# Tiles moved into the first rows of two attentions, a wait taken block by block, and a sigmoid moved by one row

## The reference, cut to what matters

```python
# first block, per layer
q, k, v, z_a, u_h, z_h, g_a, g_h = split(rms_norm(x) @ w_in)
p = softmax(q @ k.T + bias)                      # per head, two maps
o = (p[0] - lam * p[1]) @ v
y_a = rms_norm(o) * (1 - lam_init) * silu(z_a)
z = fft_long_conv(hv, filt[0]) * hx1
z = fft_long_conv(z, filt[1]) * hx2              # order 0, order 1
y_h = z * silu(z_h)
m = sigmoid(g_a) * (y_a @ w_pa) + sigmoid(g_h) * (y_h @ w_ph)
x = x + rms_norm(m @ w_out)
# second block, per layer
o_a = rmsnorm(gated_delta_rule(q, k, v, g, beta)) * silu(gz)
kv = rmsnorm(mkv) @ mla_w_ukv                    # key half kn, value half vv, per head
o_b = causal_softmax(qf @ kf.T) @ vm * silu(mz)  # eight heads, query blocks of 128
o_c = rg_lru(u) * silu(lz)
x = x + concat(o_a, o_b, o_c) @ w_out
```

## Time and profile before

| | us |
|---|---|
| median of 3 runs | 2236.86 (2232.17 to 2242.91) |
| the profiled execution | 2236.85 |
| its span, first to last instruction | 2234.8 |
| PE busy | 2137.4 |
| DVE / ACT / POOL busy | 1279.9 / 893.5 / 625.4 |
| mean granted clock of TensorE | 0.975 |

### The profile page before, as it was taken

The page is one execution under the profiler, slowest core; times in us unless marked ns, Lnnn a source line. Parts: engine busy times, 40 slices in busy tenths (PEclk is TensorE's granted clock), DMA queues, the critical chain, the costliest instruction groups (busy, mean ns, idle before and its releaser), DMA issues. The chain is left out here.

```text
span 2234.8 us, 25471 instructions
## 1 busy us (share of the span) xinstructions
PE 2137.4 (96%) x9696; PEld 1593.6 (71%) x9696; DVE 1279.9 (57%) x1988; ACT 893.5 (40%) x1406; POOL 625.4 (28%) x282
## 2 busy tenths in 40 slices
PE   8999999998999999998999999899999999989997
PEld 6777864766677864767777876677877688667776
DVE  4788845456688845456587734435155876244341
ACT  4432254433432255433473233445234633144441
POOL 2233420333323320333342300124433331001252
PEclk9999999997999999998999999999999999999999
DMA  6323321322222321322221012113232210111132
GB/s 221 103 78 104 109 66 57 125 92 85 85 92 101 118 67 48 115 88 104 78 85 57 11 41 83 38 48 108 95 123 75 69 38 20 57 38 48 57 113 85
DMA packets 48185, 180.24 MB, mean 81 GB/s; under 512 B 5728, under 2 KB 6624, under 8 KB 46658
## 3 DMA queue, kind: packets, MB, share of 16 engines
q1 hardware_dynamic: 47938, 178.49, 23.4%
q10 hardware_dynamic: 128, 0.13, 0.0%
HBM read 163.93 MB, written 14.68 MB: 80 GB/s over the span
## 5 line engine op out<-in xcount | busy, mean ns | idle before, releaser
L2383 POOL TENSOR_TENSOR w_lo<-wraw,w_hi 128x1024 fp32r<-128x1024 f32 (+1 forms) x222 | 550.6, 2482 | 1439.7 <-ACT w_hi L1150 1439.7
L1150 ACT ACTIVATE w_hi<-wraw 128x1024 fp32r<-128x1024 f32 (+1 forms) x222 | 233.7, 1053 | 692.3 <-PE bank L599 437.0
L585 PE MATMUL bank<-h_hi,w_hi 128*128 128x512 f32 (+1 forms) x1584 | 412.1, 402 | 1.1 <-ACT h_hi L1174 1.1
L594 PE MATMUL bank<-h_lo,w_hi 128*128 128x512 f32 (+1 forms) x1584 | 395.2, 392 | 0.2
L599 PE MATMUL bank<-h_hi,w_lo 128*128 128x512 f32 x1552 | 383.5, 389 | 0.0
L585 PEld LDWEIGHTS bank<-h_hi,w_hi 128*128 128x128 f32 (+1 forms) x1584 | 294.2, 189 | 95.1 <-issue 33.4
L594 PEld LDWEIGHTS bank<-h_lo,w_hi 128*128 128x128 f32 (+1 forms) x1584 | 298.3, 188 | 66.8 <-DVE h_lo L1688 1.7
L599 PEld LDWEIGHTS bank<-h_hi,w_lo 128*128 128x128 f32 x1552 | 290.1, 187 | 61.8
L702 PE MATMUL bank<-arena,wdir 128*128 128x512 f32 x256 | 114.3, 598 | 0.0
L856 PE MATMUL bank<-arena,wdir 128*128 128x512 f32 x208 | 97.6, 605 | 0.7 <-DMA wdir<-in_w_direct 0.7
L2294 DVE TENSOR_TENSOR bank<-bank,con 128x128 f32<-128x128 f32 x64 | 19.2, 299 | 132.7 <-PE bank L1068 131.6
(11 more groups left out here) (380 smaller groups left out, 3318.3 us busy)
## 6 DMA issues: line engine op xcount, KB each, us to landing
wraw<-in_w_split SPq DMA_DIRECT2D x220, 512.0 KB, 3.3
wdir<-in_w_direct SPq DMA_DIRECT2D x44, 512.0 KB, 3.3
x_park<-arena SPq DMA_DIRECT2D x3, 2048.0 KB, 6.2
arena<-x_park SPq DMA_DIRECT2D x3, 2048.0 KB, 7.9
hg_park<-arena SPq DMA_DIRECT2D x2, 2048.0 KB, 8.8
arena<-hg_park SPq DMA_DIRECT2D x2, 2048.0 KB, 8.1
arena<-bias_rows SPq DMA_DIRECT2D x2, 1792.0 KB, 7.3
arena<-in_xT SPq DMA_DIRECT2D x2, 1024.0 KB, 7.2
```

Source lines behind the costliest of these rows:

```text
L585: mm(ps[0:wd, 0:S], hi[:, k, :].bitcast(F32R), h_hi[:, k, :].bitcast(F32R), start=k == 0 and not begun, stop=False)
L594: ins = mm(ps[0:wd, 0:S], hi[:, k, :].bitcast(F32R), h_lo[:, k, :].bitcast(F32R), start=False, stop=bool(parts) and k == KT - 1)
L1150: a(w_hi[:, n % 2, 0:f].bitcast(F32R), wraw[:, n % 2, 0:f], ACT.Copy).then_inc(hi_done, 1)
L2383: nc.gpsimd.tensor_tensor(w_lo[:, n % 2, 0:f].bitcast(F32R), wraw[:, n % 2, 0:f], w_hi[:, n % 2, 0:f], ALU.subtract).then_inc(lo_done, 1)
```

## The change

1. `BESIDE_ATTENTION`: row 0 gets gh 0 and gh 1, rows 1 to 6 gh 2 to 7, rows 7 to 14 ph 0 to 7, row 15 ga 0. After the rows follow ga 1 and the last values; `BEFORE_HEAD_NORM` keeps one ga tile before each of the four row sums, and two behind.
2. ACT's sigmoid over gh comes after row 6 instead of row 7.
3. ACT runs an Exp on one column ahead of the attention's exps, and another one behind the root of the latent stage's norm.
4. The wait for all four copies before `signal_spectrum` becomes a wait per block in front of each of its products.
5. kn 4 to 7 move from behind the state loop into rows 0 to 3 of the latent attention; each is awaited by the first scores of its head.
6. The four broadcasts `nb` move behind the first two scores, each waits for the row; DVE multiplies with them in rows 0 and 1 (`norm_head`). ACT waits for the last of them before its first exps. `turned_lo` 6 and 7 move into rows 4 and 5; `turned_hi` is dealt out anew beside vv.

```diff
-BESIDE_ATTENTION = [[("gh", n)] if n < KT else [("ph", n - KT)] for n in range(H * NT)]
+BESIDE_ATTENTION = [[("gh", 0), ("gh", 1)]] + [[("gh", n)] for n in range(2, KT)] + [[("ph", n)] for n in range(KT)] + [[("ga", 0)]]
...
+for _n in range(4):
+    BESIDE_LATENT[_n] = [("kn", 4 + _n)]
...
-BEFORE_HEAD_NORM = [(1,), (2,), (3, 4), (5,), (6, 7)]
+BEFORE_HEAD_NORM = [(2,), (3,), (4,), (5,), (6, 7)]
...
@@ tensor engine: signal_spectrum
                     for n, (part, r) in enumerate(US_SUMS):
                         ps = take("us", l, o, n)
+                        pe.wait_ge(*read("ut", l, o, r))
...
-                    pe.wait_ge(*read("ut", l, o, 3))
                     signal_spectrum(o)
...
@@ tensor engine: latent attention
-                for h in range(4, MH):
-                    tile("kn", h)
                 row_sums(("on", l), [onsq[:, h, :] for h in range(H)], [("on_sq", l, h) for h in range(H)])
                 for h in range(4, MH):
                     values_tile(h)
-                for h in range(H):
+
+                def head_norm(h):
                     ps = take("nb", l, h)
-                    if h == 0:
-                        pe.wait_ge(*after("on_inv", l))
+                    pe.wait_ge(*after("on_inv", l))
                     broadcast(ps, h, 0).then_inc(filled("nb", l, h), 1)
...
                     ps = take("ms", l, h, i)
+                    if h >= 4 and i == 0:
+                        pe.wait_ge(*read("kn", l, h))
...
                 mscores(*todo[0])
                 mscores(*todo[1])
+                for h in range(H):
+                    head_norm(h)
...
@@ scalar engine: differential attention
+                link(a(small[:, 60:61], small[:, 4:5], ACT.Exp))
                 todo = [(h, i) for h in range(H) for i in range(NT)]
...
-                    if n == KT - 1:
+                    if n == KT - 2:
                         for half in range(2):
                             gates_ = PH[:, 4 * half:4 * half + 4, :]
                             a(gates_, gates_, ACT.Sigmoid).then_inc(up("gh_sig", l, half), 1)
-                keep("ga", 0)
+                keep("ga", 1)
...
@@ scalar engine: latent attention
                 turned_hi(0)
                 turned_hi(1)
-                for h in range(4, MH):
-                    keep(("kn", l, h), kn[:, h, :])
-                    turned_hi(h - 2)
+                turned_hi(2)
+                turned_hi(3)
                 row_root(("on", l), row_q, P)
+                link(a(small[:, 60:61], small[:, 4:5], ACT.Exp))
                 for h in range(4, MH):
                     keep(("vv", l, h), vn[:, h, :])
-                    if h < 6:
-                        turned_hi(h + 2)
+                    turned_hi(h)
...
+                act.wait_ge(*full("nb", l, H - 1))
                 mexps(*todo[0])
                 mexps(*todo[1])
...
@@ vector engine: latent attention
-                for h in range(H):
+
+                def norm_head(h):
+
                     dve.wait_ge(*full("nb", l, h))
                     v.scalar_tensor_tensor(oa[:, h, :], oa[:, h, :], cb("gout"), bank("nb", l, h)[:, 0:S],
                                            ALU.mult, ALU.mult).then_inc(release("nb", l, h), 1)
-                turned_lo(6)
-                turned_lo(7)
+
...
                     mweigh(h, i)
                     if n + 2 < len(todo):
                         mlogits(*todo[n + 2])
+                    if n < 2:
+                        norm_head(2 * n)
+                        norm_head(2 * n + 1)
+                    if n in (4, 5):
+                        turned_lo(n + 2)
```

More of the change, by code:

```diff
@@ L131, in psum_plan @@
             jobs += [("wt", l, h, i)] + ([("o", l, h - 1)] if i == 0 and h else [])
-        jobs += [("ga", l, 0), ("o", l, H - 1)]
+        jobs += [("ga", l, 1), ("o", l, H - 1)]
         for h in range(H):
@@ L155, in psum_plan @@
             jobs += [(g, l, j) for g, j in BESIDE_STATE[ck]]
-        jobs += [("kn", l, h) for h in range(4, MH)] + [("on", l)]
-        jobs += [("vv", l, h) for h in range(4, MH)] + [("nb", l, h) for h in range(H)]
+        jobs += [("on", l)]
+        jobs += [("vv", l, h) for h in range(4, MH)]
         todo = [(h, i) for h in range(MH) for i in range(NT)]
         for n, (h, i) in enumerate(todo):
-            jobs += ([("ms", l, h, i), ("ms", l, *todo[1])] if n == 0 else [])
+            jobs += ([("ms", l, h, i), ("ms", l, *todo[1])] + [("nb", l, j) for j in range(H)] if n == 0 else [])
             jobs += ([("ms", l, *todo[n + 2])] if n + 2 < len(todo) else [])
@@ L808, in _ @@
                         scores(*todo[n + 1])
-                    if n == KT:
-                        pe.wait_ge(*after("zh_used", l, 3))
                     for g, j in BESIDE_ATTENTION[n]:
+                        if (g, j) == ("ph", 0):
+                            pe.wait_ge(*after("zh_used", l, 3))
                         tile(g, j)
@@ L815, in _ @@
                         values(h - 1)
-                tile("ga", 0)
+                tile("ga", 1)
                 values(H - 1)
@@ L1359, in _ @@
                         exps(*todo[n + 1])
-                    if n < KT:
-                        for g, j in BESIDE_ATTENTION[n]:
+                    for g, j in BESIDE_ATTENTION[n]:
+                        if g != "ph":
                             keep(g, j)
@@ L1627, in _ @@
                     for g, j in BESIDE_LATENT[n]:
-                        keep((g, l, j), (zm if g == "mz" else zg)[:, j, :])
+                        keep((g, l, j), {"mz": zm, "gz": zg, "kn": kn}[g][:, j, :])
                     mkeep(h, i)
@@ L1911, in _ @@
                     weigh(h, i)
-                    if n >= KT:
-                        j = n - KT
+                    for g, j in BESIDE_ATTENTION[n]:
+                        if g != "ph":
+                            continue
                         dve.wait_ge(*full("ph", l, j))
```

## The result

The changed kernel takes 2224.19 us (median of 7 runs, 2223.11 to 2226.07) against 2236.86 us before: a ratio of 0.9941, with a 95% interval of 0.9930 to 0.9953. That is 12.7 us faster by the medians, 0.59%: just past the 0.5% that the prediction called measurable, though the interval reaches back across that line. Run again later beside other kernels it gave 0.9944 (0.9931 to 0.9957); one of the five executions of that set took 7483.9 us and is left out of the ratio. The profiled executions differ by 10.7 us in their spans, 2234.8 and 2224.1.

A forecast was written before the change was run, and what follows sets the result against it. TensorE, busy for 96% of the span, was taken as the bound, so only its idle or lower-clock time could be won. 1.7 + 3.0 + 8.6 - 5.1 = 8.2 us off 2236.85 gave 2228.7 us, range 2219 to 2235.

The forecast's parts named there:

- the likeliest case: Whole kernel: no change, a time within 0.5% of before (2225.7 to 2248.0 us); chance 0.62.
- the next: Whole kernel: faster than the no-change band, below 2225.7 us; chance 0.34.
- Parts 1 and 2: First attention, each layer: row 0's 2.47 us wait goes, a 1.6 us sigmoid wait comes in row 8; 1.7 us won.
- Part 3: ga tiles around the head norms: one fewer covers the chain before pa; costed at nothing, bounds 0 to 2 us per layer.
- Part 4: Order 1's spectra: block-wise waits cut PE's 2.29 us wait to 0.8, in both layers; 3.0 us won, bounds 0 to 4.6.
- Part 5: Latent attention's start: moved kn tiles cover rows 0 to 3, smaller new waits appear elsewhere; 8.6 us won at full clock.
- The clock: Lower granted clock behind new waits: one stretch per layer before `nb`, one more in both together; 3 x 1.7 = 5.1 us lost.
- The clock holds: Rival: new waits do not lower the granted clock, so 13.3 us are won, 2223.6 us; chance 0.27.
- The row-8 wait doesn't come: Rival, first attention: no new wait in row 8, 3.2 us more won, 2225.5 us; chance 0.10.
- The norm chain ends late: Rival: five ga tiles are too few, pa waits up to 2 us per layer, 4 us less, 2232.7 us; chance 0.07.
- ACT's chain to `nb` is longer: Rival, latent norm: something like a second table load delays the reciprocal, 2.6 us less won, 2231.3 us; chance 0.04.
- Slower: Rival: four new or longer waits per layer each cost 3.8 us by the clock, 30.4 us, giving 2254; chance 0.04.

The follow-up runs named there:

- row8_ga: Changed kernel with gate tile ga 0 in row 8 instead of row 15 and ph 1 to 7 in rows 9 to 15; 2221.47 us, 0.9927.
- recip_first: Changed kernel, but DVE makes only the first four `turned_lo` ahead of the norm's reciprocal, the other four in row 4; 2212.36 us, 0.9882.
- latent_only: Kernel before with only the latent attention's start changed (numbers 5, 6 and the second Exp of number 3); 2232.01 us, 0.9976.
- spectrum_only: Kernel before with only the block-wise spectrum waits (number 4); 2233.66 us, 0.9984.
- attention_only: Kernel before with only the attention's order, sigmoid and tiles (numbers 1, 2 and the first Exp of number 3); 2233.35 us, 0.9985.
- norm_early: Changed kernel, but the first head's sums stand ahead of the last head's values, so the head norms start earlier; 2225.91 us, one run.
- no_early_exp: Changed kernel without the early Exp behind the root of the latent norm; its table loads ahead of the first exponentials; 2223.30 us, one run.
- row7_ga: Changed kernel with gate tile ga 0 in row 7 instead of row 15 and the ph tiles in rows 8 to 15; 2229.72 us, 0.9962.
- best3: Changed kernel with the edits of recip_first, row8_ga and norm_early, plus weighing before the next logits in rows 5, 13, 21, 29; 2207.02 us, 0.9859.

## Why the prediction came out as it did

2224.19 us lies in the range of 2219 to 2235, 4.5 us below the likeliest 2228.7 and 1.5 us past the 2225.7 at which "no change" ended, so by the median the likeliest case (0.62) gave way to the next (0.34); the interval (to 0.9953) does not part the two. At the places that the change touches, the sum was 8.1 us against 8.2. So close an agreement is luck in part, as pa's unforeseen 1.26 us and 1.2 us more than forecast in the latent attention cancel. By its steps:

- **Parts 1 and 2** (1.7): 1.81 us measured. Row 0's wait is gone, and row 8's came at 1.58 and 1.59 us where 1.6 was worked out from the chain of copy, load, sigmoids and exps. row8_ga shows that the chain was the right cause.
- **Part 3** (nothing): wrong in two of its sentences. "The lost tile is the one between os 1 and os 2" overlooked that one more tile now stands ahead of the first head's sums: they come at 407.29 instead of 402.79, and the whole chain with them. And SP's loads were counted by the users of x, "27 us of pa tiles later"; those did not suffer, but pa's own next weights landed late behind x and the loads queued after it. It cost 1.26 us in layer 0, inside the bound of 0 to 2. In layer 1, where the filter's inputs do not follow x, there is no such wait. The rule to keep: for a load that moves, ask what else is under way then, not only who reads it.
- **Part 4** (3.0): 2.86 us, 0.65 us of wait left where 0.8 was expected.
- **Part 5** (8.6 at full clock): the parts are right one by one: 1.50, 0.69, 2.11 and 0.22 us for 1.5, 0.75, 2.2 and 0.2; the reciprocal 11.31 us after the state loop for "about 11.5"; `turned_lo(7)` 0.72 us for 0.7 (row 6 waits 2.22 us here and 1.50 in recip_first). The work at full clock was taken 0.2 us too long: the prediction's own rows give 9.64 - 0.94 - (6.64 - 1.9) = 3.96 us lost to the clock, not 3.8, and so 26.3 us of work instead of 26.5. recip_first agrees: 28.75 - 1.50 - 0.69 - 0.22 = 26.34.
- **The clock** (5.1 lost): one stretch per layer at the wait before `nb` and one in row 6, each of 1.7 us, were found as foretold, the one in row 6 of layer 0 adding 1.2 us to its 0.7. With the stretch at the lower level included, 32.85 was the forecast for the state loop to mz 0, and 32.56 and 32.51 came out.

So the terms of the change stand, and what the sum lacked is a term for everything else, which it silently put at zero: 2.6 us in the two profiled executions, 4.6 us by the medians (12.7 less 8.1). The granted clock is the largest piece of it in the traces. Over 510 to 550 us, with nearly the same work in the stretch, it was 0.67 before, 0.70 in latent_only, 0.79 after, 0.83 in spectrum_only and recip_first and 0.84 in attention_only. From before:

```profile
510.00:550.00 40.00, 34.38 (x122) 0.67 0.24 91
```

from recip_first and from norm_early:

```profile
510.00:550.00 40.00, 32.79 (x139) 0.83 0.25 93
510.00:550.00 40.00, 34.42 (x121) 0.66 0.23 88
```

norm_early has the change too, and 0.66. no_early_exp has 0.74, although its first block is the changed kernel's, instruction for instruction (0.79 there, 0.83 in recip_first). Two executions with the same instructions up to the state loop, before and latent_only, end it at 1372.38 and 1370.31. So a pair of executions can differ by 2 us in stretches without an edit, and the 2.6 us may be no more than that. The medians are firmer: by the interval the change won 10.5 to 15.7 us, more than the 8.1 at its places, which are themselves read from one execution each. Over all runs the mean clock was 0.974 for the kernel before (29 runs), 0.978 for the changed one (7) and 0.981 for recip_first (4); that mean takes in the edited places, where the 0.50 behind the 4.60 us wait is gone. Whether an edit moves the clock elsewhere, and by what, no run here shows.

One of the prediction's signs of being wrong did appear: a clock below 0.6 over more than 4 us where it wasn't, 0.51 over 1513 to 1520. As told above, spectrum_only has it without any edit to that stage.

**The rivals.** "The clock holds" named 2223.6, nearly the measured time, and its mechanism did not come true: before `nb` and in row 6 the clock fell as forecast. The right number came from elsewhere, and that is luck. "The row-8 wait doesn't come" is refuted by the row itself. "The norm chain ends late" half came true, by the queue of loads behind the norm and not by pa waiting for the norm itself. "ACT's chain to `nb` is longer" is refuted by the loads' rows. "Slower" needed 3.8 us at each new wait; they cost 1.7 beyond their length where they cost anything.

## What to carry to other kernels

When a chain of work is moved off a wait, ask what now stands ahead of it in each engine's queue: two operations of 0.69 us ahead of a reciprocal cost 3.8 us per layer here, nearly half of it by the clock. A cover tile is not only its length; the split weights, loads and GpSimd work that come with it can collide with the very step that it should cover. And in this kernel, with TensorE busy for 96%, the same instructions came 2 us apart in two executions, so a forecast of 8 us needs a term for the clock in the stretches that nobody edits, and a result needs more than one trace of each kernel before such a stretch is put down to the edit.

## What was not expected of the hardware

- A DVE operation with two inputs in SBUF stands still while GpSimd subtracts: 2.74 us instead of 0.75, ending 0.54 us after GpSimd's (348.60 and 348.06); the head norms show the same, 2.77 us for a 0.69 us product at 415.35. DVE's reciprocals of 3.35 us ran beside the same GpSimd operations without a change. The Trainium skill says so ("SBUF — State Buffer", Who interferes with whom): a DVE instruction with two SBUF inputs contends with a GpSimd one that reads SBUF, and the port pair that they share is an exclusive lock. The trace agrees; in row7_ga it made the very wait that the tile was to remove.
- A wait of some 2 us can cost nearly as much again: behind 2.11 us the granted clock was 0.76 over 7 us, part of it the lower of the two levels (1.2 GHz), and 1.00 once the wait was gone. Nor is it the wait's length alone: 1.71 us left the clock at 1.00 in one layer of no_early_exp and was followed by 0.76 in the other; 1.43 us in one piece (best3, row 7) left it at 1.00, and 1.50 + 0.38 us (recip_first, rows 6 and 7) did not.
